# Three pads in SBUF and one constant fewer: new start addresses for the operands of a float32 transformer kernel

## The reference

```python
# first block: modulation, one wide projection, three branches, feed-forward
mod_l = split(silu(c) @ w_mod + b_mod, 6);  mod_c = split(silu(c_ctx) @ w_mod + b_mod, 6)
zl  = modulate(rms_norm(x), ...) @ w_in + b_in            # 2048 -> 13312 columns
zkv = modulate(rms_norm(ctx), ...) @ w_in[:, K:G] + b_in  # keys and values of the context
mix = g_conv * conv(zl) + g_sgu * sgu(zl) + g_att * neighbourhood_attention(zl, zkv)
x = x + mod_l[2] * (mix @ w_o + b_o)
x = x + mod_l[5] * (square(relu(modulate(rms_norm(x)) @ w_ff1 + b_ff1)) @ w_ff2 + b_ff2)
x = rms_norm(x)
# second block: 16 meta tokens are put in front, 272 tokens
lam = exp(sum(lq1 * lk1)) - exp(sum(lq2 * lk2)) + lam_init
h = h + rms_norm(diff_attention(rms_norm(h) @ attn_w_in, lam) @ attn_w_out)
h = h + rms_norm(pool_mixer(rms_norm(h) @ pool_w_in, w_group) @ pool_w_out)
return h[:, 16:]
```

## The kernel before, in words

| tensor | start | start modulo 256 | start modulo 64 | from tile to tile |
|---|---|---|---|---|
| `cst` | 19520 | 64 | 0 | |
| `vt` | 23008 | 224 | 32 | |
| `AH`, `AL` | 41440, 58848 | 224 | 32 | 1088 bytes |
| `raw0` to `raw3` | 76256 and on | 224 | 32 | |
| `hi0` to `hi4` | 92640 and on | 224 | 32 | 512 bytes |
| `lo0` to `lo4` | 113120 and on | 224 | 32 | 512 bytes |
| `G16` | 152992 | 160 | 32 | |
| `BH`, `BL` | 169376, 177568 | 160 | 32 | 1024 bytes |
| `YL`, `YH` | 194528, 211936 | 224 | 32 | 1088 bytes |
| `CL`, `CH` | 196576, 212960 | 224 | 32 | 1024 bytes |

## Time and profile before

### The profile page before, as it was taken

How to read it: one execution, slowest core, us unless ns; L and a number is a source line. 1 busy time by engine, 2 the same in 40 slices (tenths; PEclk the granted TensorE clock), 3 DMA queues, 4 the chain that set the end, 5 groups by cost and what they waited for, 6 DMA issues and landing times.

```text
span 2867.4 us, 51278 instructions
## 1 busy us (share of the span) xinstructions
PE 2733.7 (95%) x21330; PEld 2574.7 (90%) x21330; DVE 1915.3 (67%) x2964; ACT 1224.9 (43%) x1801; POOL 219.4 (8%) x212
## 2 busy tenths in 40 slices
PE   5889999899999899999999999999999998979996
PEld 1279977699999899999999999999999997979996
DVE  6655567789999777875554555677656665477564
ACT  2122244444434544544443444564444444444452
POOL 4000011200003200100000000021000000220011
PEclk8999999999999999999999999999999999989998
DMA  7766643264877687775555555554444443535553
GB/s 259 267 211 219 210 145 115 84 221 155 268 238 256 199 278 254 262 230 194 188 186 183 183 185 185 183 192 155 155 133 159 148 156 108 188 110 177 185 190 103
DMA packets 163991, 539.01 MB, mean 188 GB/s; under 512 B 31024, under 2 KB 35120, under 8 KB 163632
## 3 DMA queue, kind: packets, MB, share of 16 engines
q1 hardware_dynamic: 163760, 535.73, 56.7%
HBM read 533.57 MB, written 2.10 MB: 187 GB/s over the span
## 4 chain that ended last, share of the span: by engine, by line
PE 84%; DVE 10%; issue 2%; DMA 1%; ACT 1%; SPq 1%; POOL 0%; POOLq 0%; ACTq 0%; DVEq 0%
PE ps L472 26%; PE ps L477 25%; PE ps L474 25%; DVE lo L1529 3%; PE ps L573 2%; PE ps L626 1%; PE ps L645 1%; DMA raw<-in_w_mod 1%; DVE macc L1646 1%; DVE CV L1789 1%; PE ps L634 1%; DVE row L2075 1%; DVE macc L1517 0%; DVE macc L1520 0%; PE ps L800 0%
## 5 line engine op out<-in xcount | busy, mean ns | idle before, releaser
L472 PE MATMUL ps<-AH,hi 128*128 128x256 f32 (+2 forms) x4480 | 1289.0, 288 | 13.5 <-DVE AL L2151 13.5
L477 PE MATMUL ps<-AH,lo 128*128 128x256 f32 (+2 forms) x4480 | 1277.6, 285 | 19.6 <-DVE lo L1529 19.6
L474 PE MATMUL ps<-AL,hi 128*128 128x256 f32 (+2 forms) x4480 | 1274.1, 284 | 0.0
L923 ACT ACTIVATE hi<-raw 128x1024 fp32r<-128x1024 f32 x808 | 850.5, 1057 | 935.0 <-PE ps L477 498.4
L1529 DVE TENSOR_TENSOR lo<-raw,hi 128x1024 fp32r<-128x1024 f32 x808 | 977.9, 1224 | 191.5 <-ACT hi L923 190.3
L472 PEld LDWEIGHTS ps<-AH,hi 128*128 128x128 f32 x4480 | 850.6, 190 | 45.3 <-issue 34.5
L477 PEld LDWEIGHTS ps<-AH,lo 128*128 128x128 f32 x4480 | 851.3, 190 | 23.0 <-DVE lo L1529 22.8
L474 PEld LDWEIGHTS ps<-AL,hi 128*128 128x128 f32 x4480 | 850.2, 190 | 0.8
L472 PE MATMUL ps<-YH,hi 128*128 128x256 f32 (+1 forms) x1536 | 434.0, 283 | 6.5 <-DVE YL L2086 6.5
L477 PE MATMUL ps<-YH,lo 128*128 128x256 f32 (+1 forms) x1536 | 435.1, 283 | 0.0
L474 PE MATMUL ps<-YL,hi 128*128 128x256 f32 (+1 forms) x1536 | 435.1, 283 | 0.0
(11 more groups left out here) (245 smaller groups left out, 2606.6 us busy)
## 6 DMA issues: line engine op xcount, KB each, us to landing
raw<-in_w_ff SPq DMA_DIRECT2D x256, 512.0 KB, 4.2
raw<-in_w_in SPq DMA_DIRECT2D x208, 512.0 KB, 4.4
raw<-in_w_mod SPq DMA_DIRECT2D x192, 512.0 KB, 4.6
raw<-in_w_ain SPq DMA_DIRECT2D x128, 512.0 KB, 3.5
raw<-in_w_pin SPq DMA_DIRECT2D x64, 512.0 KB, 3.5
raw<-in_w_o SPq DMA_DIRECT2D x32, 512.0 KB, 4.6
raw<-in_w_aout SPq DMA_DIRECT2D x32, 512.0 KB, 3.5
raw<-in_w_pout SPq DMA_DIRECT2D x32, 512.0 KB, 3.5
```

The lines of the kernel that those rows point to most:

```text
L472: e.matmul(b.ap[:, o], hi[:, k, :], xh, start=start and k + i == 0, stop=False, skip_group_check=many)
L474: e.matmul(b.ap[:, o], hi[:, k, :], xl, start=False, stop=False, skip_group_check=many)
L477: mm = e.matmul(b.ap[:, o], los[j % NSPLIT][:, k, :], xh, start=False, stop=stop and k == KU - 1, skip_group_check=many)
L923: e.activation(his[u % NSPLIT][:, :, :], raws[i % NRAW][:, :].rearrange("p (k m) -> p k m", k=KU), ACT.Copy).then_inc(s_hi, 1)
```

## The change

Three pads of 32, 64 and 480 bytes are put in, at the left ahead of `H`, at the left ahead of `G16`, and at the right ahead of everything there. `onesf` (512 bytes) is gone: the matmul of the lambda takes `ones[2048]`, whose entries are 1/2048, and the exponent's scale of 2048 takes that back. No instruction is added or moved; one memset is removed. Afterwards `AH`, `AL`, `raw`, `hi`, `lo`, `G16`, `BH`, `BL`, `YH`, `YL`, `CH`, `CL` begin at multiples of 256, and the tiles of `AH`, `AL`, `YH`, `YL` at 64k modulo 256. `cst` and `vt` stay where they are. At the tightest point no byte is free.

```diff
         vt = sb("vt", [128, 256])
+        sb("pad0", [128, 8])
         H = sb("H", [128, 16, L])
...
         ones = {n: sb(f"ones{n}", [128, 128]) for n in (2048, 1024, 256)}
-        onesf = sb("onesf", [128, 128])
         macc = [sb(f"macc{i}", [128, 512]) for i in range(2)]
+        sb("pad1", [128, 16])
         G16 = sb("G16", [128, 16 * T])
 
+        sb("pad2", [128, 120], F32, ctx, "right")
         early, first = ExitStack(), ExitStack()
...
-            e.matmul(XB[:, 0:2], onesf[:, :], vt[:, LAMC:LAMC + 2], start=True, stop=True).then_inc(s_lamp, 1)
+            e.matmul(XB[:, 0:2], ones[2048][:, :], vt[:, LAMC:LAMC + 2], start=True, stop=True).then_inc(s_lamp, 1)
...
-            e.activation(vt[:, LAMC + 2:LAMC + 4], XB[:, 0:2], ACT.Exp).then_inc(s_lame, 1)
+            e.activation(vt[:, LAMC + 2:LAMC + 4], XB[:, 0:2], ACT.Exp, scale=2048.0).then_inc(s_lame, 1)
...
-            e.memset(onesf[:, :], 1.0)
```

## The result

The change makes no gain. Median 2877.81 us (2872.23 to 2884.09, 20 runs) against 2872.99 us (2868.22 to 2879.36, 20 runs) of the kernel before beside it: ratio **1.0016**, 95% interval 1.0009 to 1.0023. The prediction was 2783 us, range 2705 to 2866, and had put 0.80 on faster. What came true is the time of rival D, plus 4.8 us.

The account below looks back on a forecast made before the run. TensorE was taken as the bound, matmul count times distance of starts. Step 2's 110.8 us less 21 us lost gives 90 us off 2869.2, so 2779; plus 3.5 to the median, 2783 us, range 2705 to 2866.

Parts of the forecast that it names:

- rival D: Change does nothing to the engine: 6.7 ns are a constant of this type, the surcharge stays; 2872.65 us, chance 0.11.
- Step 2: Large matmuls on TensorE: aligned starts save one 64-byte block, 6.67 ns each at 256 and 272 columns; 110.8 us in all.
- A: Likeliest case for TensorE's large matmuls: the extra block goes, the surcharge stays; 2783 us, chance 0.42.
- Step 3: Matmuls on `AH` and `YH`, whose tiles wander by 64 bytes: their 5 ns surcharge was left as it is.
- quiet pace: Matmuls of 256 columns on `BH`: 113.3 ns, without the 5 ns surcharge; losing it would cost 5.8 us, counted as nothing.
- worst triple: Three matmuls of 258 columns taking 0.38 us, 126.7 ns each against 119.6; bound of 7.1 ns more for the surcharge.
- Step 1: Memset, constant and scale: the 0.17 us memset is hidden behind the load of `vec` and worth nothing.
- Step 4: Stretches where TensorE isn't the only bound: 21 us of the saving lost, bounds 5 and 45 us.
- Step 5: Transfers, with `raw` moved to multiples of 256: nothing counted, 2 us either way.
- E: Slower: weights and moving operands begin at one place modulo 256 and their reads meet more often; 2911 us, chance 0.09.
- B: Both the extra block and the surcharge go from TensorE's large matmuls; 2731 us, chance 0.23.
- lower floor: Case B with a floor of 106.7 ns for 256 columns: another 44 us would go, 2687 us.

Follow-up runs that it names:

- the bare stream: Kernel of its own, 96 matmuls per arrangement, nothing else running, stepping places of tiles against weights: 256 columns take 113.3 to 120.0 ns over sixteen starts.
- the bare stream with lengths varied: The stream of matmuls alone again, with moving columns from 64 to 512 and weight columns varied: 111.7 ns from 128 to 240 moving columns against 128 weight columns.

## Why the prediction was wrong

**What bounds the kernel** was right. TensorE is the bound and its time is the number of matmuls times their distance: paces that were moved on purpose moved the median, by 1.8% down at best and by 0.4% up at worst.

**Step 2, the extra block, is the step that failed.** It put 110.8 us on a block of 64 bytes that a start at 32 modulo 64 was taken to touch in addition. Measured: a shift of all operands by 32 bytes is worth nothing (113.4 and 113.4, 120.0 and 119.8 ns in the bare stream), the paces of `AH` and `YH` stayed, and with `BH` put back the ratio is 0.9998. The argument had two holes that could be seen in the rows. First, that 6.67 ns equal 16 columns was a match of one number, and no row varied the absolute start while the rest stood still. Second, it read the difference of `BH` and `YH` as "the address of the moving operand", which is true, and then took a part that both have in common to be an address effect too, for which nothing spoke. Rows 8 and 9 could not tell a constant of the engine from a block, and rival D, which said so, got 0.11 where the rows gave it as much as A.

**Step 3, the surcharge,** was right for what it left alone: the wandering paces stayed to 0.1 ns. It also named the one effect that the change has, that `BH` loses its quiet pace when it comes level with the weights, and counted it as nothing because only the first triple of the earlier trace rows showed it. It cost 6.7 ns in the steady pace rather than 5, and 5.6 ns over whole units, 6.4 us on TensorE; 4.8 us reached the median, and the experiment on `BH` alone returned it all. Why the rest does not reach the end was not tried; VectorE is busy 138 of the 146 us there. The bound that this step took from the worst triple is a reading of rounded starts: 0.38 us / 3 is 126.7 ns, the unrounded starts give 125.3, so 5.7 ns over the mean and not 7.1.

**Step 1** held: one memset fewer, and nothing at the end. **Step 4** had nothing to take a share of. **Step 5** held: the DMA share of 704 to 850 is 0.77 against 0.78.

**The rivals.** D has the time, not the reason: it held that addresses do nothing, and they do, up to 6.7 ns a matmul in steps of 16 bytes, but only against each other. E's reason, weights and tiles that meet at one place, is real in sign for `BH`; its price on all the rest was wrong, because for the rest no relative place moved. The prediction had written that itself as the argument against E, and it was equally the argument against A: what the change holds constant, the relative places, is what the rows showed to matter. The lower end of the range was said to lie two fifths of the way from B, 2731, to its lower floor, 2687; 2705 is three fifths of the way, which changes nothing here. The signs that it set out worked: "if all paces stay, D holds" read the result from four pairs of starts.

**What stays open.** Which part of the engine makes the pace depend on these places; why the sixteen starts in steps of 16 bytes have no simple order; what sets 113.3 ns at 256 columns, since neither the columns nor the weight load does; and what in an interruption chooses between 113.3 and 117.8 ns. The runs measure these, they do not explain them.

## What to carry to other kernels

Before pricing an effect of an address, ask whether the rows vary it in absolute terms or against another operand, and what the change holds constant. Where TensorE is the bound with a weight load per matmul and fp32r operands, read the distance of starts for each operand; if they differ at one size, a bare stream that steps the places costs one short run and gives the table. Here that table was worth 1.8%: tiles at a constant place, 192 bytes above the high weights modulo 256, the low weights 128 bytes from the high ones, and where tiles have to wander, their low parts 128 bytes from their high parts.

## What the runs showed of the hardware

- The pace of fp32r matmuls of 256 columns with a load of 128 weight columns each runs from 113.3 to 120.0 ns over sixteen relative places of tiles and weights, and up to 123.3 ns at a place that is no multiple of 16 bytes (place 4); moving all operands together by 32 bytes changes nothing (113.4 and 113.4 ns).
- One arrangement can have two steady paces, 113.3 and 117.8 ns, and kept one, in these traces, until something interrupted the stream.
- A load of 128 weight columns holds the distance at 111.7 ns for 128 to 240 moving columns; 64 weight columns, and 32, with 128 moving ones give 60.0 ns.
- In the bare stream with lengths varied, matmuls of 64 columns began at 42.6 us, and no gap stood between any two matmuls from there on. They ran 111.7 ns apart at the full granted clock until 46.4 us, and 213.3 ns apart at the 1.2 GHz level from then on. Those of 128 columns that followed stood at it too, 213.3 ns each. Those of 192 columns began under it at 121.0 us, and from 124.9 us on the clock was full again. The windows of this kernel (columns as above without DVE):

```profile
43.00:46.00 3.00, 3.00 (x29) 3.00 (x29) 0.00 (x0) 0.00 (x0) 1.00 0.00 0
54.00:79.00 25.00, 25.00 (x119) 25.00 (x119) 0.00 (x0) 0.00 (x0) 0.50 0.00 1
80.00:120.00 40.00, 40.00 (x189) 40.00 (x189) 0.00 (x0) 0.00 (x0) 0.50 0.00 1
126.00:133.00 7.00, 7.00 (x65) 7.00 (x65) 0.00 (x0) 0.00 (x0) 1.00 0.00 0
```

The clock is the third figure from the end: 1.00 with 64 columns at first, 0.50 with 64 and with 128, 1.00 with 192. TensorE is shown busy without a pause in all four. In the first bare stream 192 matmuls of 128 columns that followed others of 256 at the full clock kept it (111.7 ns).
